# Two networks on one core: the first context pass takes its dense products in plain float32

## The reference

```python
hc = modulate(rmsnorm(xc, norm1_g[l]), csh1, csc1)
pc = hc @ w_in[l]                                  # 36 tiles of 128 features
q_c, k_c, v_c = (split_heads(u) for u in jnp.split(pc[..., GLU_END:QKV_END], 3, axis=-1))
yc_conv = conv_branch(pc[..., :GLU_END], ...)      # 31-tap depthwise conv, layernorm, silu, @ w_conv_out
yc_attn = merge_heads(context_attention(q_c, k_c, v_c)) @ w_na_out[l]
xc = xc + cg1 * gated_merge(pc[..., QKV_END:], yc_conv, yc_attn, w_out[l])
hc2 = modulate(rmsnorm(xc, norm2_g[l]), csh2, csc2)
xc = xc + cg2 * conv_ffn(hc2, w_up[l], ffn_dw[l], ffn_dw_b[l], w_down[l])
```

## Time and profile before

| | |
|---|---|
| median of 3 runs | 3338.27 us (3336.58 to 3340.38) |
| the profiled execution | 3346.49 us, its span 3344.3 us |
| granted PE clock, mean | 0.925 of full |
| PE busy | 2899.1 us, 87% of the span |
| POOL, DVE, ACT busy | 1531.5, 1768.0, 1231.6 us |
| c0 on PE: first dense record to last residual add | 1153.54 to 1642.58 us |

### The profile page before, as it was taken

The page is one execution under the profiler, slowest core; times in us unless marked ns, Lnnn a source line. Parts: engine busy times, 40 slices in busy tenths (PEclk is TensorE's granted clock), DMA queues, the critical chain, the costliest instruction groups (busy, mean ns, idle before and its releaser), DMA issues.

```text
span 3344.3 us, 44321 instructions
## 1 busy us (share of the span) xinstructions
PE 2899.1 (87%) x15992; PEld 2353.6 (70%) x15992; DVE 1768.0 (53%) x2143; ACT 1231.6 (37%) x1778; POOL 1531.5 (46%) x773
## 2 busy tenths in 40 slices
PE   6999845899999786689798897999988898899997
PEld 6966522677778675689776676877876666677876
DVE  6864644245333467654549765523334987452424
ACT  4444211233232343354424632523343354243423
POOL 3441200233444397457567634343454765334443
PEclk9988967899999898899899998999998999999999
DMA  4335655422332233335432112222332212222221
GB/s 171 97 101 184 203 154 154 122 77 68 100 99 89 80 117 107 101 119 171 138 96 72 60 59 92 82 90 80 107 108 87 73 65 65 75 77 94 94 95 69
DMA packets 125811, 342.47 MB, mean 102 GB/s; under 512 B 37216, under 2 KB 45536, under 8 KB 125024
## 3 DMA queue, kind: packets, MB, share of 16 engines
q1 hardware_dynamic: 96800, 321.71, 30.0%
q10 hardware_dynamic: 28864, 18.76, 1.9%
HBM read 330.61 MB, written 7.45 MB: 101 GB/s over the span
## 4 chain that ended last, share of the span: by engine, by line
PE 63%; DVE 16%; DVEq 6%; ACT 4%; issue 3%; DMA 3%; POOLq 2%; POOL 1%; SPq 1%; ACTq 0%
PE ps L264 33%; PE ps L282 19%; DVE co L1869 4%; DVEq L1870 3%; PE ps L1977 2%; PE ps L579 2%; POOLq L1960 2%; DVE nacc L359 1%; DVE mv L2032 1%; DMA wraw<-w_ada 1%; ACT whi L221 1%; DVE sm L1845 1%; DVE pex L1854 1%; DMA yf<-s_y 1%; POOL wlo L229 1%
## 5 line engine op out<-in xcount | busy, mean ns | idle before, releaser
L229 POOL TENSOR_TENSOR wlo<-wraw,whi 128x1024 fp32r<-128x1024 f32 x493 | 1214.6, 2478 | 1691.0 <-ACT whi L221 1690.3
L221 ACT ACTIVATE whi<-wraw 128x1024 fp32r<-128x1024 f32 x493 | 518.1, 1054 | 635.8 <-PE ps L282 269.8
L264 PE MATMUL ps<-xhi,whi 128*128 128x512 f32 (+2 forms) x1728 | 565.9, 350 | 7.8 <-DVE fa L2089 4.5
L264 PE MATMUL ps<-xlo,whi 128*128 128x512 f32 (+2 forms) x1728 | 564.4, 349 | 0.0
L264 PE MATMUL ps<-xhi,wlo 128*128 128x512 f32 (+2 forms) x1728 | 354.3, 349 | 7.4 <-POOL wlo L229 7.4
L264 PEld LDWEIGHTS ps<-xhi,whi 128*128 128x128 f32 x1728 | 317.8, 189 | 54.2 <-ACT whi L221 5.5
L264 PEld LDWEIGHTS ps<-xlo,whi 128*128 128x128 f32 x1728 | 318.1, 189 | 43.8
L264 PEld LDWEIGHTS ps<-xhi,wlo 128*128 128x128 f32 x1728 | 282.2, 189 | 51.9 <-POOL wlo L229 8.3
L1869 DVE SCALAR_TENSOR_TENSOR co<-ub,vec,co 128x512 f32<-128x512 f32 (+1 forms) x234 | 294.1, 1296 | 6.1 <-issue 0.4
L264 PE MATMUL ps<-hhi,whi 128*128 128x512 f32 (+1 forms) x616 | 223.1, 369 | 4.3 <-DVE gt L2029 3.3
L264 PE MATMUL ps<-hlo,whi 128*128 128x512 f32 (+1 forms) x616 | 222.4, 368 | 0.0
(11 more groups left out here) (322 smaller groups left out, 4973.8 us busy)
## 6 DMA issues: line engine op xcount, KB each, us to landing
wraw<-stream SPq DMA_DIRECT2D x493, 512.0 KB, 3.4
wraw<-w_ada SPq DMA_DIRECT2D x96, 512.0 KB, 4.7
biasb<-attn_bias ACTq DMA_DIRECT2D x32, 256.0 KB, 3.2
xin<-x0T SPq DMA_DIRECT2D x4, 528.0 KB, 7.0
s_u<-uk ACTq DMA_DIRECT2D x8, 264.0 KB, 4.0
res<-x0T ACTq DMA_DIRECT2D x1, 2048.0 KB, 8.9
s_y<-yk ACTq DMA_DIRECT2D x64, 32.0 KB, 1.8
yf<-s_y SPq DMA_DIRECT2D x8, 256.0 KB, 4.7
```

Of the source, the lines that this page charges most:

```text
L221: act.activation(whi[:, s], wraw[:, s], ACT.Copy).then_inc(hi_done[s], 1)
L229: pool.tensor_tensor(wlo[:, s], wraw[:, s], whi[:, s].bitcast(F32), ALU.subtract).then_inc(lo_done[s], 1)
L264: last = pe.matmul(ps[:, bank, 0:b - a], w[:, s, kt], x[:, kt, c0 + a:c0 + b], start=start, stop=stop)
```

## The change

For c0's 120 units (`whole(g)`) neither weights nor inputs are split. PE multiplies `wraw` with `x1`, `h1` or `m1`, float32 tiles in the places of `xhi`, `hhi` and `mhi`: eight matmuls for a unit, not 24. With that go c0's `split_hi` on ACT and `split_lo` on POOL, the `lo` subtractions on DVE and the `hi` copies on ACT (except the writes that now give `x1`, `h1`). PE waits for `landed` in place of `hi_done` and `lo_done`, and SP loads a slot's next unit after `unit_done`, not after the splits. ACT and POOL split l0's first four units at c0's end as before. The core of the diff:

```diff
+WHOLE = (N_B1, N_B1 + N_LAYER)
...
+    x1 = at("x1", [P, NT, TM], O_X)
+    h1 = at("h1", [P, NT, SEQ], O_HH)
...
     def split_hi(act, g, i=0, rb=0):
-        if g >= N_UNITS:
+        if g >= N_UNITS or whole(g):
             return
...
+    def here(pe, g, i, rb):
+        pe.wait_ge(landed[slot(g, i, rb)[0]], (raw_round(g, i, rb) + 1) * 16)
...
     def pe_unit(pe, g, i, rb, xh, xl, T, nk=8, dual=False, wide=False, c0=0):
-        hi_split(pe, g, i, rb)
+        (here if whole(g) else hi_split)(pe, g, i, rb)
         pe.wait_ge(acc_free[s], rnd + 1)
...
+        if whole(g):
+            for kt in range(nk):
+                last = product(wraw, xh, kt, kt % 4 == 0 if dual else kt == 0, kt % 4 == 3 if dual else kt == nk - 1)
+            last.then_inc(unit_done[s], 1)
+            return
...
     # pe_quad
+        if whole(g):
+            for kt in range(tail):
+                if hi is not None:
+                    hi(pe, kt)
+                for j in range(R):
+                    if kt == 0:
+                        here(pe, g + j, i, rb)
+                        pe.wait_ge(acc_free[slot(g + j, i, rb)[0]], slot(g + j, i, rb)[1] + 1)
+                    product(j, wraw, xh, kt, start=kt == 0)
+            for j in range(R):
+                for kt in range(tail, nk):
+                    ...
+                last.then_inc(unit_done[slot(g + j, i, rb)[0]], 1)
+            return
...
     # norm_dve, one=True
             dve.wait_ge(n_hi.sem, n_hi.past("hi", h0 + kt))
+            if one:
+                continue
...
     # mix_act: the conv branch's silu
+            if p.one:
+                act.activation(h1[:, m, 0:T], lsq[:, m, 0:T], ACT.Silu, bias=colr(f"lnb{p.l}", 1, m)).then_inc(p.c_h.sem, 1)
+                continue
...
     # merge_dve
+                if p.one:
+                    dve.tensor_tensor(m1[:, m, 0:T], gc, ga, ALU.add).then_inc(p.m_w.sem, 1)
+                    continue
...
     # ffn_act, behind the last chunk, and ffn_dve
+            if p.one and t0 + n == FF2_TILES:
+                for j in range(R):
+                    split_hi(act, WHOLE[1] + j)
...
+                    if p.one:
+                        dve.wait_ge(p.f_s.sem, p.f_s.past("silu", t))
+                        dve.tensor_tensor(h1[:, i * 2 + j, 0:T], fs[:, j, 0, 0:T], fa[:, j, 0, 0:T], ALU.mult).then_inc(p.f_w.sem, 1)
+                        continue
...
             def load(g, row, i=0, rb=0):
-                if g >= R:
-                    sp.wait_ge(lo_done[s], raw_round(g, i, rb))
+                if whole(g - R):
+                    sp.wait_ge(unit_done[s], slot(g, i, rb)[1] + 1)
+                elif g >= R:
+                    sp.wait_ge(lo_done[s], freed_round(g, i, rb))
                 sp.dma_start(wraw[:, s], A["stream"][row]).then_inc(landed[s], 16)
```

More of the change, by code:

```diff
@@ L283, in product @@
             return last
+        if whole(g):
[9 more added lines that the diff above has]
+                for kt in range(tail, nk):
+                    if j == 0 and hi is not None:
+                        hi(pe, kt)
+                    last = product(j, wraw, xh, kt, stop=kt == nk - 1)
+                last.then_inc(unit_done[slot(g + j, i, rb)[0]], 1)
+            return
         for kt in range(tail):
@@ L359, in norm_add, with norm_act @@
             dve.tensor_tensor(a, a, nsq[:, kt % 2, 0:T], ALU.add).then_inc(n_acc.sem, 1)
-    def norm_act(act, n, T, eps, split=True, shift=None, dst=None, sums=6):
+    def norm_act(act, n, T, eps, split=True, shift=None, dst=None, sums=6, one=False):
         act.wait_ge(n_sum.sem, n_sum.past("sum", n))
@@ L392, in norm_rows_pe, with norm_dve @@
         last.then_inc(n_row.sem, 1)
-    def norm_dve(dve, n, src, T, gain, split=True, shift=None, dst=None):
+    def norm_dve(dve, n, src, T, gain, split=True, shift=None, dst=None, one=False):
         dve.wait_ge(n_root.sem, n_root.past("root", n + (1 if n else 0)))
@@ L1599, in pe_filler @@
         s, rnd = slot(g)
-        hi_split(pe, g, 0, 0)
+        (here if p.one else hi_split)(pe, g, 0, 0)
         pe.wait_ge(acc_free[s], rnd + 1)
@@ L1603, in pe_filler @@
         o = ps[:, s % 2, 0:p.T]
+        if p.one:
+            for kt in range(NT):
+                last = pe.matmul(o, wraw[:, s, kt], x1[:, kt, 0:p.T], start=kt == 0, stop=kt == NT - 1)
+            last.then_inc(unit_done[s], 1)
+            return
         for kt in range(NT):
@@ L1898, in mix_dve @@
                 scale_dve(dve, p, n)
-            if out_due(p, n) is not None:
+            if out_due(p, n) is not None and not p.one:
                 out_lo_dve(dve, p, out_due(p, n))
@@ L1927, in mix_dve @@
             dve.scalar_tensor_tensor(lsq[:, m, 0:T], cn[:, m, 0:T], colr(f"lng{l}", 1, m), ps[:, 7, 0:T], ALU.mult, ALU.mult).then_inc(p.c_n.sem, 1)
-        for m in range(4):
+        for m in range(0 if p.one else 4):
             dve.wait_ge(p.c_h.sem, p.c_h.past("hi", m))
@@ L1977, in product @@
             return pe.matmul(ps[:, s + R * (kt // 4), 0:p.T], w[:, s, kt], x[:, kt, 0:p.T], start=start, stop=stop)
+        hh = whole_of(p, hhi)
         def attention_part(g):
+            if p.one:
+                here(pe, g, 0, 0)
+                for kt in range(4, 8):
+                    product(g, wraw, hh, kt, start=kt == 4, stop=kt == 7)
+                return
             hi_split(pe, g, 0, 0)
@@ L1996, in merge_pe @@
             pe.wait_ge(p.c_h.sem, p.c_h.past("hi", kt))
+            if p.one:
+                for j in range(R):
+                    last = product(M + j, wraw, hh, kt, start=kt == 0, stop=kt == 3)
+                    if kt == 3:
+                        last.then_inc(unit_done[(M + j) % R], 1)
+                continue
             for j in range(R):
@@ L2071, in ffn_act @@
             loop(act, n // 2, body)
-            if p.after is None or t0 + n < FF2_TILES:
+            if p.one and t0 + n == FF2_TILES:
+                for j in range(R):
+                    split_hi(act, WHOLE[1] + j)
+            elif p.one:
+                continue
+            elif p.after is None or t0 + n < FF2_TILES:
                 act_units(act, D, 2)
@@ L2344, in _ @@
                     mix_pool(pool, p)
-                    pool_units(pool, p.U + 36, 20 if p is passes[-1] else 21)
+                    if p.one:
+                        for j in range(R):
+                            split_lo(pool, WHOLE[1] + j)
+                    else:
+                        pool_units(pool, p.U + 36, 20 if p is passes[-1] else 21)
 def consts():
```

98 lines of the change are left out of this document (69 added, 29 removed).

## The result

| | before | after |
|---|---|---|
| median | 3338.27 us (9 runs, 3333.05 to 3343.31) | 3320.7 us (9 runs, 3312.7 to 3331.26) |
| ratio, with its interval of 95% | | 0.9948 (0.9931 to 0.9964) |
| the profiled execution, its span | 3346.49, 3344.3 us | 3327.92, 3325.9 us |
| c0, first dense record to last residual add | 489.0 us | 469.3 us |
| of it up to the feed-forward's first quad | 266.4 us | 223.9 us |

The kernel is 17.6 us faster by the medians, 0.52%; forecast were 16.3. The two halves of c0 go opposite ways: 42.5 us are gained up to `w_out`, 22.8 are given back in the feed-forward.

What follows compares the result with a forecast made beforehand. c0 was taken as paced in turn by POOL, DVE, ACT and PE; rebuilt from PE's side, 410 + 22 + 14 + 17.5 + 10.4 = 474 us against 489, with 1.8 less ahead: -16.8, so 3322 us, range 3306 to 3345.

Steps and rivals of the forecast that it cites:

- record: One plain float32 record of 256 columns on PE takes 0.217 us, with 0.213 and 0.2265 as ends.
- 1. dense records: PE's 1888 plain records in c0 at 0.217 us take 410 us (before, 2832 at 0.119 take 337).
- 2. attention beside the fillers: PE's attention work in c0's filler stage takes 20 us, with gaps 22.
- 3. waits that stay: PE's waits in c0 for free accumulators, mean and centring, variance and row, and the norm before the feed-forward: 14 us.
- 4. load waits: New PE waits for raw weights around c0's quads, as slots reload only once PE has finished them: 17.5 us.
- 5. half clock: PE at half clock at c0's first quad, merge, feed-forward and three w_down quads, 1.7 us each: 10.4 us.
- ahead of c0: Before c0, POOL no longer splits beside the previous norm's last two sums: 1.8 us less.
- The first rival: A PE record takes 0.239 us, a split record's excess belonging to every pass: c0 515, time 3362 us; chance 0.10.
- the second's first half: PE's records in c0 take 0.2265 us each: +18, so 3339 us; the whole rival's chance 0.14.
- The second's other halves: Loads of 4.7 us, not 3.6, add 12 us, or half clock behind all eleven c0 waits some 9; chance 0.14.
- The third rival, DVE's tail: DVE's taps in c0 are slow for their own sake and the mean stays late: 20 us lost, 3342; chance 0.06.
- The fourth, the feed-forward's handshake: The up units' handshake stays at 13.4 us for four and adds to PE: 10 us, 3332; within the base case.

Runs made afterwards that it cites:

- short_loads: The changed kernel with c0's units loading two of their eight input tiles (128 KB for 512 KB): 3311.28 us, ratio 0.9905.
- pool_busy: The changed kernel with an unread subtraction of a split's size on POOL before each of its 21 taps in c0: 3339.72 us, ratio 1.0001.
- extra_up: The changed kernel with a ninth product (two plain records) in each of 40 up units of c0's feed-forward: 3336.45 us, ratio 0.9991.
- after_again: The changed kernel, unaltered, run again on another chip: 3323.02 us against 3339.4 of before on that chip, ratio 0.9945.
- mix_whole: The changed kernel with plain products only in c0's 52 units up to w_out, its feed-forward split as before: 3303.41 us, ratio 0.9891.
- ffn_whole: The changed kernel with plain products only in the 68 units of c0's feed-forward, the first 52 split as before: 3363.95 us, ratio 1.0065.

## Why the prediction was right, step by step

The forecast was 3322 us and the median is 3320.7; c0 was to be 474 us and is 469.3. That the median came within 1.3 us is in part luck. c0 and its head gained 22.3 us where 16.8 were forecast, and the rest of the execution, for which nothing was forecast, was 4 to 5 us longer. The terms of the sum, against the trace after:

| term | forecast | measured |
|---|---|---|
| record | 0.217 us | 41.72 / 192 = 0.217 |
| 1. dense records | 410 | 1888 x 0.2167 = 409 |
| 2. attention beside the fillers | 22 | 94.6 - 352 x 0.2167 = 18.3 |
| 3. waits that stay | 14 | 1.3 + 2.3 + 3.4 + 5.1 = 12.1 |
| 4. load waits | 17.5 in 11 places | 18.6 in 11 |
| 5. half clock | 10.4 | 11.2 is left over; the windows' clocks give 9.7, the quads' records 9.1 |
| sum | 474 | 469.3 |
| ahead of c0 | -1.8 | -2.6 |

- **The record.** It decided the case. The first rival fell by it, and so did the second's first half: 0.217, not 0.239 or 0.2265. The second's other halves fell by the loads (3.4 to 3.8 us from their issue, not 4.7) and by the clock (four slow quads, not eleven). What a split record takes over its columns does not belong to each pass.
- **Attention beside the fillers** was 3.7 us too high. The 22 held 2 for gaps, and there are 1.2 us of them in 94.6. The other 2.9 fit a slip of the reading: the 20 were left of a window with a clock of 0.93 whose dense records were all priced at full clock, so they held time at half clock too. After the change the clock there is 1.00, and 17.1 are left. This, the 1.9 of the waits that stay and 0.9 of the records are 6.5 us less; loads and clock took 1.9 back.
- **Waits that stay.** Mean and centring 2.3 (2.5 forecast), variance and row 3.4, 1307.95 to 1311.30 (3.5), the norm 5.1, 1372.04 to 1377.17 (5.8), free accumulators 1.3 before the fillers (1.3) and 0.6 before the gates (0.9), which is counted with the filler stage.
- **Load waits.** The number and the places are as forecast, and the mechanism too: 3.5 to 4.0 us from the release of a slot to PE's start (3.6 forecast), covered only by what PE still has to do. The longest is 2.75 us, where 2.3 was forecast before a quad. `short_loads` shows that they cost what they last.
- **Half clock.** The size is right by two errors that cancel. The forecast had six places at 1.7 us, which is 10.2 and not 10.4; that 1.7 stands in none of its rows. The trace has four, at more each: 52 records in 14.38 us at c0's first quad, 46 in 11.89 at `w_out`, 52 in 13.36 at the feed-forward's first quad and 46 in 11.90 at one of `w_down`. Against 0.2167 a record they lost 3.1, 1.9, 2.1 and 1.9 us, 9.1 together. Merge and two `w_down` quads, where the forecast had a loss, ran at 1.00. By the windows it is 9.7 (lengths by what each clock lacks of 1.00: 33.3 x 0.09, 38.5 x 0.08, 17.1 x 0.11, 19.0 x 0.09). What made one `w_down` quad slow and not the others is open.
- **The third rival, DVE's tail,** is excluded: DVE was done at 1289.9 (1294 forecast), the gates ended at 1302 (1303), and DVE waited for PE. `pool_busy` shows why the forecast's side of it was right: with POOL's load put back, the mean comes 17 us later (165.8 us behind c0's first record, 148.7 after the change), and the kernel's whole gain is gone.
- **The fourth, the feed-forward's handshake,** is excluded by 13.9 us for four up units, forecast to the tenth, and by `extra_up`.
- **Last residual add:** 1622.5, forecast near 1626.

Ahead of c0, from the last residual add of 512 columns (1132.94, 1130.64 before) to c0's first record are 20.3 us, 22.9 before. The sums that are behind it took this, after:

```profile
1132.94 0.69 DVE L982 TENSOR_TENSOR res<-res,ps 128x512 f32<-128x512 f32 x1 [3.97 <-PE ps L283]
1133.72 1.48 DVE L400 TENSOR_TENSOR nacc<-nacc,nsq 128x512 f32<-128x512 f32 x2
```

1.48 us for two, 3.14 in the earlier trace rows, where 1.3 was the estimate; no row gave the part of a tap that doubles with its columns. The sums account for 1.7 of the 2.6 us. c0 and its head together are 22.3 us shorter in the two profiles, and the spans differ by 18.4: the residual add before it came 2.3 us later, and the part behind c0 was 1.6 longer. In `after_again` that part is 5.4 us shorter than in the first profile of the same kernel, so differences of this size occur between executions (there on another chip) and say nothing of the change.

What the forecast did not say is where its 15 us would come from. It put the two halves in one sum; from its own terms one could have had them apart. The second half has 528 products: 1056 records x 0.217 = 229, loads 10.9, half clock 4 x 1.7 = 7, together 247 us against 222.6 before (1419.98 to 1642.58). That is 24 us more, and 22.8 were measured; for the first half 227 us are left, 39 less, and 42.5 were measured. As to why: the first half has 416 products and the second 528, each 0.077 us dearer (0.434 for 0.357), 32 and 41 us more for PE. The first half saved 53 us of PE's idle time, and its busy time grew by only 10 us, since time at half clock went too (0.86 to 0.97). The second saved 9 us of idle time, and its busy time grew by 31. For the second, `mix_whole` has the split form and the kernel after the plain one: 41 us of products more, 20.3 of waits for `fa` less, 11.5 of the load waits more, and a clock of 0.99 in place of 0.94 (223.9 x 0.06 less 245.3 x 0.01, 11 us less). That sums to 21, and 245.3 - 223.9 is 21.4. With the two sums in hand the first half alone would have been the better change to try, before any run.

## What to carry to other kernels

A trade of splits for plain products is a trade between engines, and is worth taking stage by stage: where another engine paces (POOL in the fillers, DVE at the taps) PE's dearer product costs nothing, where PE paces already (`w_down`) it is paid in full, and where its new time passes the other engine's (13.9 against 13.4 us for four up units) in part. Before costing such a change, split the stretch at the places where the pacing engine changes and make one sum for each; a small total can be the difference of two large terms. Freeing a slot later (by PE's end, not by a copy's) costs the load's latency at each place where several slots are wanted at once, and memory that the change sets free can buy it back.

## What the runs showed of the hardware that was not expected

- A plain float32 record of 256 columns, which by its time streams them twice, takes 0.2167 us (69.35 / 320), 3.4 ns over 512 columns at 2.4 GHz; a split record takes 0.119, 12.6 ns over its 256. The Trainium skill (TensorE: Matmul & The Clock Gate, Wait — 56ns, not 53.3ns?) gives about 2.5 ns over N columns at 2.4 GHz. Taken with 512 columns that is 215.8 ns, near the plain record; with 256 it is 109.2, and the split record is 10 ns over it; both are estimates from the page's figure.
- A load of 512 KB lands 3.4 us after its issue, one of 128 KB after 2.2 (`short_loads`). By these two points, an estimate, 1.6 us of the 3.4 go with the bytes and 1.8 don't.
- Executions differ ahead of c0: its first record starts at 1144.4 (`extra_up`) to 1157.7 us (`ffn_whole`) in profiles of kernels whose code up to there is the same but for the splits beside the last norm; c0's own length repeated to 0.1 us in the changed kernel (469.3 and 469.2).
